# Softmax heads: q and k staged apart from V, DMA copies queued ahead of the weight load

## The chip, the core and the metric

The kernel runs on one core of a Trainium2 chip. The metric is the time of one execution on the device, in microseconds, from the first to the last instruction of the core. A core has TensorE (matmuls; its granted clock is 2.4 or 1.2 GHz), ScalarE, VectorE, GpSimd and SyncE, each with a queue of its own that it works off in order; they meet through semaphores.

## What is computed

One token sequence of 512 with width 1024 goes through a first block (stick-breaking attention with 8 heads, softmax attention with 8 heads and latent projections, "mla", gates, output projection) and two further layers, of which the first has a softmax attention with 16 heads and a forget term, "fox". The change touches both softmax attentions.

```python
def fox_attention(h, w_in, b_f, w_out):
    ...
    q = q * jnp.asarray(HEAD_DIM ** -0.5, q.dtype)
    f_logit = (proj[..., 3 * D:] + b_f).astype(jnp.float32)
    log_f = jax.nn.log_sigmoid(f_logit)
    c = lax.cumsum(log_f, axis=1).transpose(0, 2, 1)
    ...
        s = jnp.einsum('bhqd,bhkd->bhqk', qb, k, preferred_element_type=jnp.float32)
        s = s + cb[..., :, None] - c[..., None, :]
        q_pos = start + jnp.arange(Q_BLOCK)
        s = jnp.where(k_pos[None, :] <= q_pos[:, None], s, NEG_INF)
        pr = jax.nn.softmax(s, axis=-1)
        return jnp.einsum('bhqk,bhkd->bhqd', pr.astype(v.dtype), v)
```

The mla attention has the same form without the forget term, with 96 features for q and k, and a mask by chunks of 64.

## The kernel before

**Precision.** Every float32 operand is split into a high part, which ScalarE makes by casting to fp32r, and a low part, which VectorE makes by subtracting the high part from the value. A product is then three matmuls: high x high, high x low, low x high (L724 to L726, the helper `three`).

**Weights.** SyncE loads weight units of 1 MB into two raw slots (`load`, L490 to L494), in the order of a table. A load waits (L492, L493) until VectorE has split the unit that lay in the slot. In the attention stages the unit's two splits are cut into shares: w0 and w1 on ScalarE (L1214), c0 to c3 on VectorE (L1687); c0 waits for w1. Unit p+1 is split in pair p.

**Attention, in pairs of heads.** The softmax attentions work on two heads at a time, 4 pairs in mla and 8 in fox. `hh` 0 is the even head of a pair, 1 the odd one. Each engine follows an order written out by hand, a string of steps (`PE_FOX`, `ACT_FOX`, `DVE_FOX` and so on, the last two fox pairs `PE_LAST`, `ACT_LAST`, `DVE_LAST`). A step is a letter and a number:

- TensorE: z0 to z7 the score tiles (z0 to z3 of the even head, z4 to z7 of the odd one, L984 and L988), t0 to t7 the turns of the exponentials (L996), v0 and v1 the product with V, g0 to g7 the shares of a projection that runs beside the attention (6 matmuls a share).
- ScalarE: e0 to e7 exponentials (L1431), p0 to p7 high parts of the turned tiles (L1448), r0 and r1 inverse of the sums (L1438, L1440), w0 and w1 weight shares, s1 and s2 the staging of a head, o the output's high parts (L1371).
- VectorE: m0 to m7 row maxima (L2019), p0 to p7 low parts (L1723), g0 and g1 the output of a head (L1889), x0 and x1 the projection's output (L1879), c0 to c3 weight shares, s1 and s2 staging.

A score tile s uses PSUM bank s mod 3, so t(s) comes before z(s+3); v0 needs p3, v1 needs p7 of both ScalarE and VectorE; t(s) needs e(s) and VectorE's p(s-2).

**Staging** (`stage`, L1303 to L1318 on ScalarE, from L1833 on VectorE). Before a head's scores its q and k are cast (two ACTIVATE), then its V (a third); VectorE subtracts three times. q and k lie in one of two slots: the even head's in `head_qk`, the odd head's in spare rows of `act_b` (the other way round in mla). A slot is free when the scores of the head two before are done. V's place is free when the product with V of the head two before is done; ScalarE waits for it between the casts of k and V. s1 stages the odd head of this pair at the pair's start, s2 the even head of the next pair in its middle.

**Fox only: `copy_halves`** (L639 to L648). A head has 64 features; the free half of the partitions carries a second copy of the high part, and two rows carry the forget term. SyncE issues four DMAs a head: two of 64 x 512 (L645) and two of one row from `ssum` (L648). TensorE waits for all four before the head's first score tile (L975). The loop at L663 to L670 issues, for each pair, the copies of its odd head, the weight load that this pair allows, and the copies of the next even head.

Of the kernel before, what the change touches and what calls it, by code (L numbers as in the profile page):

```python
# [2394 lines left out]
```

## Time and profile before

| | us |
|---|---|
| median of 3 runs | 1895.83 |
| lowest and highest | 1895.67 and 1896.23 |
| the profiled execution | 1897.7 |
| its span, first to last instruction | 1895.9 |
| TensorE busy in it | 1770.2 (93%) |
| VectorE busy | 1069.8 (56%) |
| ScalarE busy | 739.6 (39%) |
| mean granted clock of TensorE | 0.975 of full |

The mla attention lies between about 325 and 414 us of the span, the fox attention between 567 and 804 us. Times in the rows below are counted from the span's start. A busy share is an average over stages with different limits; what ends a stage is read from the waits inside it. A timeline row merges equal instructions in a row (x2) and shows in brackets how long its engine was idle before it and what ended that.

### The profile page before, as it was taken

What the parts mean: (1) busy time and instruction counts of PE and PEld (TensorE: products, weight loads), DVE (VectorE), ACT (ScalarE), POOL (GpSimd) and SP (SyncE); (2) the same over time, 40 slices, a digit from 0 to 9 for tenths busy, and PEclk for the clock granted to TensorE, in tenths of its full rate; (3) what the DMA queues carried; (4) which work ended last, traced back from release to release, by engine and by line L of the source; (5) the groups of instructions that cost most, each with busy time, mean ns of one, the idle gap of its engine ahead of it and who ended that gap; (6) DMA issues with size and microseconds to landing.
All of it is one profiled execution on the core that took longest, in us unless ns stands there. A gap on an engine that the chain in (4) does not pass through costs nothing.

```text
span 1895.9 us, 22068 instructions
## 1 busy us (share of the span) xinstructions
PE 1770.2 (93%) x8332; PEld 1456.2 (77%) x8332; DVE 1069.8 (56%) x1394; ACT 739.6 (39%) x1073; POOL 179.3 (9%) x144
## 2 busy tenths in 40 slices
PE   8999999999897677899999999989999999999987
PEld 6978876888696566677888888667887788888866
DVE  6467767765555445667353444667555735444465
ACT  4266673663324434544122222453123412122245
POOL 2001110001200000022000000331002200000031
PEclk9999999999998888899999999989999999999999
DMA  7312123124231211213322322232231332232221
GB/s 241 98 45 66 58 58 100 45 69 132 67 96 40 60 41 39 73 56 111 103 97 89 109 91 78 67 100 94 89 106 56 111 108 93 89 111 89 78 68 66
DMA packets 166059, 160.48 MB, mean 85 GB/s; under 512 B 15137, under 2 KB 158782, under 8 KB 165726
## 3 DMA queue, kind: packets, MB, share of 16 engines
q1 hardware_dynamic: 165982, 159.42, 26.9%
q8 instruction: 52, 0.85, 0.2%
q14 instruction: 25, 0.20, 0.0%
HBM read 150.36 MB, written 4.19 MB: 82 GB/s over the span
## 4 chain that ended last, share of the span: by engine, by line
PE 68%; issue 12%; DVE 7%; POOL 4%; ACT 4%; DMA 3%; SPq 1%; POOLq 0%; DVEq 0%; ACTq 0%
PE bank L724 21%; PE bank L726 21%; PE bank L725 21%; POOL ssum L2325 3%; PE bank L984 2%; PE bank L996 1%; DMA head_qk<-ssum 1%; DVE split_weights L1679 1%; DVE work L1738 1%; DVE act_b L1723 1%; POOL tmp L2358 1%; DVE act_a L1725 1%; ACT split_weights L1205 1%; PE bank L988 1%; DMA raw_weights<-in_w_mlp_up 1%
## 5 line engine op out<-in xcount | busy, mean ns | idle before, releaser
L724 PE MATMUL bank<-act_a,split_weights 128*128 128x512 f32 x1392 | 558.1, 401 | 27.9 <-DVE act_a L1725 27.5
L726 PE MATMUL bank<-act_a,split_weights 128*128 128x512 f32 x1392 | 548.2, 394 | 0.0
L725 PE MATMUL bank<-act_a,split_weights 128*128 128x512 f32 x1392 | 548.1, 394 | 0.0
L1205 ACT ACTIVATE split_weights<-raw_weights 128x2048 fp32r<-128x2048 f32 (+1 forms) x119 | 223.7, 1880 | 345.3 <-PE bank L726 345.3
L1679 DVE TENSOR_TENSOR split_weights<-raw_weights,split_weights 128x2048 fp32r<-128x2048 f32 (+1 forms) x119 | 275.6, 2316 | 123.9 <-ACT split_weights L1205 120.5
L724 PEld LDWEIGHTS bank<-act_a,split_weights 128*128 128x128 f32 x1392 | 264.8, 190 | 93.8 <-issue 23.0
L726 PEld LDWEIGHTS bank<-act_a,split_weights 128*128 128x128 f32 x1392 | 263.9, 190 | 57.9
L725 PEld LDWEIGHTS bank<-act_a,split_weights 128*128 128x128 f32 x1392 | 264.6, 190 | 54.1 <-issue 2.2
L724 PE MATMUL bank<-act_b,split_weights 128*128 128x512 f32 x664 | 260.4, 392 | 0.0
L725 PE MATMUL bank<-act_b,split_weights 128*128 128x512 f32 x664 | 258.4, 389 | 0.0
L726 PE MATMUL bank<-act_b,split_weights 128*128 128x512 f32 x664 | 258.4, 389 | 0.0
L2329 POOL TENSOR_TENSOR ssum<-sq 128x512 f32<-128x512 f32 x16 | 28.0, 1749 | 1289.5 <-ACT sq L1235 1286.1
L725 PEld LDWEIGHTS bank<-act_b,split_weights 128*128 128x128 f32 x664 | 124.6, 188 | 27.0 <-issue 1.2
L724 PEld LDWEIGHTS bank<-act_b,split_weights 128*128 128x128 f32 x664 | 124.6, 188 | 26.8 <-issue 1.2
L726 PEld LDWEIGHTS bank<-act_b,split_weights 128*128 128x128 f32 x664 | 124.6, 188 | 26.0
L1547 ACT ACTIVATE act_b<-tmp 128x512 fp32r<-128x512 f32 x64 | 40.3, 632 | 229.2 <-DVE tmp L2186 227.9
L1235 ACT ACTIVATE sq<-work 128x512 f32<-128x512 f32 x117 | 71.0, 625 | 147.7 <-DVE work L2205 58.1
L2325 POOL TENSOR_TENSOR ssum<-ssum,sq 128x512 f32<-128x512 f32 x77 | 109.0, 1416 | 157.5 <-ACT sq L1235 149.2
L2186 DVE SCALAR_TENSOR_TENSOR tmp<-bank,rstd 128x512 f32<-128x512 f32 x64 | 43.5, 690 | 137.2 <-PE bank L726 136.2
L2205 DVE TENSOR_TENSOR work<-bank,work 128x512 f32<-128x512 f32 x48 | 32.9, 691 | 120.0 <-PE bank L726 120.0
L2019 DVE TENSOR_REDUCE negmax<-bank 128x1 f32<-128x128 f32 (+1 forms) x96 | 45.7, 485 | 77.0 <-PE bank L988 76.8
L1723 DVE TENSOR_TENSOR act_b<-tmp,act_b 128x512 fp32r<-128x512 f32 (+3 forms) x136 | 77.4, 603 | 10.7 <-ACT act_b L483 9.3
(188 smaller groups left out, 2081.1 us busy)
## 6 DMA issues: line engine op xcount, KB each, us to landing
raw_weights<-in_w_mlp_up SPq DMA_DIRECT2D x32, 1024.0 KB, 5.4
raw_weights<-in_w_mlp_down SPq DMA_DIRECT2D x32, 1024.0 KB, 5.1
raw_weights<-in_w_in SPq DMA_DIRECT2D x20, 1024.0 KB, 5.4
raw_weights<-in_w_conv_in SPq DMA_DIRECT2D x12, 1024.0 KB, 5.1
raw_weights<-in_w_attn_in SPq DMA_DIRECT2D x16, 512.0 KB, 4.7
raw_weights<-in_w_ple_gate SPq DMA_DIRECT2D x8, 1024.0 KB, 5.1
raw_weights<-in_w_out SPq DMA_DIRECT2D x4, 1024.0 KB, 5.1
raw_weights<-in_w_attn_in SPq DMA_DIRECT2D x4, 1024.0 KB, 5.2
```

Source lines behind the costliest of these rows:

```text
L724: nc.tensor.matmul(dst, w[0], a[0], start=first, stop=False)
L725: nc.tensor.matmul(dst, w[0], a[1], start=False, stop=False)
L726: mm = nc.tensor.matmul(dst, w[1], a[0], start=False, stop=last)
L984: nc.tensor.matmul(dst, qk(a)[0:width, j * P:(j + 1) * P], qk(b)[0:width, 0:cols], start=pass_ == 0, stop=False)
L1205: nc.scalar.activation(wsp[:, pl.slot, 0, pl.split_cols], raw[:, pl.slot, pl.raw_cols], ACT.Copy)\
L1235: nc.scalar.activation(sq[:, parity, :], src, ACT.Square).then_inc(sq_done, 1)
L1547: nc.scalar.activation(act_b[:, 0, 2 * j + m, :], tmp[:, m, :], ACT.Square)\
L1679: V.tensor_tensor(wsp[:, pl.slot, 1, cols], raw[:, pl.slot, pl.raw_cols], wsp[:, pl.slot, 0, cols].bitcast(F32), ALU.subtract).then_inc(w_ ...
L1723: V.tensor_tensor(dst, src, hi.bitcast(F32), ALU.subtract).then_inc(sem_, 1)
L2019: V.reduce_max(negmax[:, s:s + 1], score_bank(s, last)[:, 0:(s % TT + 1) * P], AX, negate=True)\
L2186: V.scalar_tensor_tensor(out=tmp[:, m, :], in0=done(pl, m)[:, :], scalar=0.0, in1=rstd[:, :], op0=ALU.max, op1=ALU.mult).then_inc(tile_rea ...
L2325: nc.gpsimd.tensor_tensor(ssum[:, :], ssum[:, :], sq[:, parity, :], ALU.add).then_inc(sq_added, 1)
```

## The change

It does three things. (1) The staging of q and k is a step of its own, that of V another. s2 and s3 stage q and k of the next pair's even and odd head as soon as the scores in the slot are done (z3 and z7); y1 and y2 stage V of this pair's odd head and of the next pair's even head. V gets semaphores of its own (`v_hi`, `v_staged`), for which the product with V waits. The first two heads' q and k are staged before the stage's loop. (2) `copy_halves` issues two DMAs a head in place of four: one for both copies (its source and target are two parts each, by `both_parts`) and one for the two rows. For that q's low part in fox goes to the other half of its slot. (3) In SyncE's loop the copies of the next even head stand ahead of the weight load, those of the next odd head behind it. All order strings of mla and fox are new but `PE_LAST`.

```diff
-        HI_STEPS = {"sb": 4, "mla": 3, "fox": 3}
+        HI_STEPS = {"sb": 4, "mla": 2, "fox": 2}
...
+        PE_MLA = "z0 g0 z1 g1 z2 t0 z3 t1 z4 g2 t2 z5 t3 z6 g3 v0 t4 z7 g4 t5 t6 g5 t7 g6 g7 v1"
+        ACT_MLA = "e0 e1 y1 p0 e2 p1 w0 e3 p2 p3 s2 w1 e4 e5 p4 y2 e6 p5 e7 p6 r0 p7 s3 r1"
...
-        PE_FOX = "z0 z1 z2 g0 g1 t0 z3 t1 g2 z4 t2 t3 z5 g3 t4 v0 z6 t5 z7 g4 g5 t6 t7 g6 g7 v1"
-        ACT_FOX = "s1 e0 e1 p0 e2 p1 e3 p2 p3 e4 e5 s2 p4 p5 w0 e6 e7 r0 p6 p7 w1 r1"
-        DVE_FOX = "m0 m1 m2 s1 m3 p0 p1 m4 p2 p3 m5 s2 m6 p4 m7 p5 c0 c1 g0 p6 p7 x0 c2 x1 c3 g1"
+        PE_FOX = "z0 z1 g0 g1 z2 t0 z3 t1 z4 g2 t2 g3 t3 z5 g4 t4 z6 z7 v0 t5 g5 t6 t7 g6 g7 v1"
+        ACT_FOX = "w0 e0 e1 w1 p0 e2 p1 s2 e3 e4 p2 y1 p3 e5 s3 e6 p4 p5 e7 r0 p6 y2 p7 r1"
+        DVE_FOX = "m0 m1 c0 c1 m2 p0 m3 m4 p1 c2 s2 c3 p2 p3 m5 m6 m7 y1 p4 p5 g0 p6 p7 x0 y2 x1 s3 g1"
...
-        ACT_LAST = ("s1 e0 e1 e2 o0 p0 w0 e3 o1 p1 p2 o2 w1 e4 e5 p3 s2 e6 p4 r0 e7 p5 p6 p7 o3 r1",
+        ACT_LAST = ("e0 e1 e2 y1 o0 p0 w0 e3 o1 p1 p2 o2 s2 w1 e4 e5 p3 e6 p4 s3 r0 e7 p5 y2 p6 p7 o3 r1",
...
+        def both_parts(hh, second):
+
+            if hh:
+                rows = act_b[:, :, 4:6, :]
+                return rows[:, :, 0, :] if second == 2 else act_b[:, :, :, :].rearrange("p a k n -> p (a k) n")[:, 4:14:9, :]
+            return head_qk[:, 0:second + 1:second, :]
...
-                qk, (own, other) = qk_parts("fox", hh), halves(hh)
+                own, other = halves(hh)
                 sp.wait_ge(ATT["fox"]["stage_hi"], HI_STEPS["fox"] * h + 2)
-                for dst, src in ((qk(0)[other, :], qk(0)[own, :]), (qk(3)[own, :], qk(2)[own, :])):
-                    sp.dma_start(dst.bitcast(F32), src.bitcast(F32)).then_inc(halves_copied[hh], 16)
-                for part in range(2):
-                    row, to = 32 * part + h, other.start + part
-                    sp.dma_start(qk(3)[to:to + 1, :].bitcast(F32), ssum[row:row + 1, :]).then_inc(halves_copied[hh], 16)
+                dst, src = both_parts(hh, 3)[other, :, :], both_parts(hh, 2)[own, :, :]
+                sp.dma_start(dst.bitcast(F32), src.bitcast(F32)).then_inc(halves_copied[hh], 16)
+                sp.dma_start(qk_parts("fox", hh)(3)[own.start:own.start + 2, :].bitcast(F32), ssum[h:h + 33:32, :])\
+                    .then_inc(halves_copied[hh], 16)
...
             copy_halves(0)
+            copy_halves(1)
             load_qk(Place(tab, "fox_qk_next", 2), 4)
-            for pair in range(FOX_HEADS // 2):
-                copy_halves(2 * pair + 1)
+            for pair in range(FOX_HEADS // 2 - 1):
+                copy_halves(2 * pair + 2)
                 if pair < 3:
                     load_qk(Place(tab, "fox_qk_next", 3 + pair), 5 + pair)
                 elif pair < 5:
                     load_out(Place(tab, "fox_out", pair - 3), pair - 3)
-                if pair < FOX_HEADS // 2 - 1:
-                    copy_halves(2 * pair + 2)
+                copy_halves(2 * pair + 3)
...
                 def values(i, hh):
                     pe.wait_ge(A["pt_ready"], 8 * i + 4 * hh + 4)
                     pe.wait_ge(A["gathered"], FREE + 2 * i + hh)
+                    pe.wait_ge(A["v_staged"], 2 * i + hh + 1)
```

SyncE's queue at pair 0, where `fox_qk_next` 3 is loaded: `raw_weights` is the load (two issues), `act_b` the odd head's slot, `head_qk` the even head's. Before:

```order
L494 DMA raw_weights<-in_w_attn_in 128x8x128 [waits w_split]
L494 DMA raw_weights<-in_w_attn_in 128x8x128
L645 DMA head_qk<-head_qk 64x512 [waits fox_stage_hi]
L645 DMA head_qk<-head_qk 64x512
L648 DMA head_qk<-ssum 1x16x32 x2
L645 DMA act_b<-act_b 64x512 [waits fox_stage_hi]
L645 DMA act_b<-act_b 64x512
L648 DMA act_b<-ssum 1x16x32 x2
```
After, the same load and its neighbours:

```order
L652 DMA head_qk<-head_qk 64x2x512 [waits fox_stage_hi]
L653 DMA head_qk<-ssum 2x512
L501 DMA raw_weights<-in_w_attn_in 128x8x128 [waits w_split]
L501 DMA raw_weights<-in_w_attn_in 128x8x128
L652 DMA act_b<-act_b 64x2x512 [waits fox_stage_hi]
L653 DMA act_b<-ssum 2x512
```
Before, the copies of both heads of the next pair stand behind the load that waits for `w_split`; now the even head's stand ahead of it and the odd head's behind it, two issues a head for four.

ScalarE in a fox pair, the staging of the next even head: L1312 and L1313 cast q and k, L1318 V, L1448 is a p step. Before (s2 p4 p5):

```order
L1308 ISA
L1312 ISA [waits fox_scores]
L1312 ACTIVATE head_qk<-work 64x512
L1313 ISA
L1313 ACTIVATE head_qk<-work 64x512
L1318 ISA [waits fox_out]
L1318 ACTIVATE head_v<-work 128x4x64
L1446 REGISTER_ALU [waits fox_turned]
L1448 ACTIVATE act_b<-bank 128x128 [waits fox_out]
L1448 ACTIVATE act_b<-bank 128x2x128 [waits fox_turned]
```
After, the staging of the next odd head (L1319, L1320), which did not exist here, ahead of e6, p4, p5 and e7 (s3 e6 p4 p5):

```order
L1315 ISA
L1319 ISA [waits fox_scores]
L1319 ACTIVATE act_b<-work 64x512
L1320 ISA
L1320 ACTIVATE act_b<-work 64x512
L1442 REGISTER_ALU
L1443 ACTIVATE tmp<-bank,negmax 128x384 [waits fox_negmax]
L1458 REGISTER_ALU [waits fox_turned]
L1460 ACTIVATE act_b<-bank 128x128 [waits fox_out]
L1460 ACTIVATE act_b<-bank 128x2x128 [waits fox_turned]
```
V's cast with its wait for `fox_out` no longer stands behind those of q and k; the wait of s3 for `fox_scores` (z7) stands ahead of e6.

VectorE in a fox pair: L1687 (after: L1706) is a c step. Before (m7 p5 c0 c1 g0 p6 p7), L2019 an m step, L1889 a g step, near the pair's end:

```order
L2019 TENSOR_REDUCE negmax<-bank 128x1 [waits fox_scores]
L1723 TENSOR_TENSOR act_b<-bank,act_b 128x2x128 [waits fox_pt_hi]
L1685 REGISTER_ALU
L1687 TENSOR_TENSOR split_weights<-raw_weights,split_weights 128x512 [waits w_hi]
L1687 TENSOR_TENSOR split_weights<-raw_weights,split_weights 128x512
L1884 REGISTER_ALU
L1889 TENSOR_TENSOR work<-bank,sq 64x512 [waits fox_sum_inverse,fox_out]
L1723 TENSOR_TENSOR act_b<-bank,act_b 128x3x128 [waits fox_pt_hi]
L1723 TENSOR_TENSOR act_b<-bank,act_b 128x4x128 [waits fox_pt_hi]
```
After, at the pair's start (m0 m1 c0 c1 m2 p0 m3):

```order
L2043 TENSOR_REDUCE negmax<-bank 128x1 [waits fox_scores]
L2042 REGISTER_ALU
L2043 TENSOR_REDUCE negmax<-bank 128x1 [waits fox_scores]
L1704 REGISTER_ALU
L1706 TENSOR_TENSOR split_weights<-raw_weights,split_weights 128x512 [waits w_hi]
L1706 TENSOR_TENSOR split_weights<-raw_weights,split_weights 128x512
L2042 REGISTER_ALU
L2043 TENSOR_REDUCE negmax<-bank 128x1 [waits fox_scores]
L2048 REGISTER_ALU
L1742 TENSOR_TENSOR act_b<-bank,act_b 128x128 [waits fox_pt_hi]
L2042 REGISTER_ALU
L2043 TENSOR_REDUCE negmax<-bank 128x1 [waits fox_scores]
```
The first two c steps, which wait for `w_hi` (w1 on ScalarE), moved from ahead of g0, p6 and p7 to ahead of m2.

## Rows read from the trace of the kernel before

**Rows 1.** Waits of TensorE, 560 to 757 us: waiter, releaser, us, times, longest.

```profile
PE bank L984 <- DMA head_qk<-ssum: 38.8, 5, 8.2
PE bank L724 <- DVE act_b L1723: 11.6, 6, 1.9
```

**Rows 2.** Stretches: length, busy us of each engine (instructions), granted clock, DMA share, GB/s.

```profile
325.15:414.30 89.15, 88.68 (x495) 76.38 (x496) 61.62 (x122) 55.35 (x110) 0.00 (x0) 1.00 0.14 45
567.43:757.02 189.59, 139.17 (x696) 118.48 (x697) 92.49 (x179) 84.39 (x166) 0.00 (x0) 0.86 0.17 45
757.02:804.00 46.98, 37.31 (x193) 30.80 (x192) 28.94 (x57) 27.98 (x59) 0.00 (x0) 0.89 0.26 74
```

**Rows 3.** Waits of SyncE's queue, 560 to 800 us, columns as in Rows 1.

```profile
SPq L493 <- DVE split_weights L1687: 126.1, 5, 27.2
```

**Rows 4.** Timeline of SyncE's queue: start, us, line, DMA, count.

```profile
657.99 1.00 SPq L494 DMA_DIRECT2D raw_weights<-in_w_attn_in  x2
...
660.72 1.24 SPq L648 DMA_DIRECT2D head_qk<-ssum  x2
...
744.96 1.14 SPq L645 DMA_DIRECT2D head_qk<-head_qk  x2
```

**Rows 5.** DMA issues of the whole run: count, KB each, median us to landing.

```profile
head_qk<-head_qk SPq DMA_DIRECT2D x16, 128.0 KB, 4.8
...
head_qk<-ssum SPq DMA_DIRECT2D x16, 2.0 KB, 4.1
act_b<-ssum SPq DMA_DIRECT2D x16, 2.0 KB, 2.3
```

**Rows 6.** Timeline of TensorE, pair 1 and two later starts: start, us, line, [idle before].

```profile
632.05 0.80 PE L984 MATMUL bank<-head_qk 128*128 128x256 f32 x2 [7.99 <-DMA head_qk<-ssum]
...
643.98 0.48 PE L724 MATMUL bank<-act_b,head_v 128*128 128x512 f32 x1
...
646.00 0.51 PE L984 MATMUL bank<-act_b 128*128 128x384 f32 x2
...
655.66 0.49 PE L724 MATMUL bank<-act_b,head_v 128*128 128x512 f32 x1 [1.93 <-DVE act_b L1723]
...
666.06 0.79 PE L984 MATMUL bank<-head_qk 128*128 128x256 f32 x2 [8.21 <-DMA head_qk<-ssum]
...
757.02 0.40 PE L984 MATMUL bank<-head_qk 128*128 128x256 f32 x2
```

**Rows 7.** Stretches from z0 to t0, columns as in Rows 2; last the five after a wait.

```profile
567.43:571.48 4.05, 4.05 (x22) 3.50 (x23) 3.07 (x6) 2.15 (x5) 0.00 (x0) 1.00 0.29 65
...
632.05:638.79 6.74, 6.74 (x22) 5.75 (x22) 3.07 (x6) 0.84 (x2) 0.00 (x0) 0.56 0.00 0
...
sum 31.96, PE 31.95 PEld 27.41 DVE 15.37 ACT 4.20 POOL 0.00; mean PE 6.39 PEld 5.48 DVE 3.07 ACT 0.84 POOL 0.00
```

**Rows 8.** Timeline of ScalarE in pair 1, columns as in Rows 6.

```profile
644.46 0.62 ACT L1312 ACTIVATE head_qk<-work 64x512 fp32r x1
...
646.30 0.42 ACT L1318 ACTIVATE head_v<-work 128x256 fp32r x1 [0.70 <-PE bank L726]
...
648.12 1.16 ACT L1431 ACTIVATE tmp<-bank,negmax 128x384 f32<-128x384 f32 x2
649.31 0.60 ACT L1438 ACTIVATE sq<-bank 64x512 f32<-64x512 f32 x1
...
650.59 1.00 ACT L1448 ACTIVATE act_b<-bank 128x384 fp32r<-128x384 f32 x2
651.49 1.05 ACT L1214 ACTIVATE split_weights<-raw_weights 128x1024 fp32r<-128x1024 f32 x1
```

**Rows 9.** Timeline of VectorE in pair 1, columns as in Rows 6.

```profile
652.58 1.29 DVE L1687 TENSOR_TENSOR split_weights<-raw_weights,split_weights 128x512 fp32r<-128x512 f32 x2 [3.69 <-ACT split_weights L1214]
...
654.39 1.14 DVE L1723 TENSOR_TENSOR act_b<-bank,act_b 128x384 fp32r<-128x384 f32 x2
...
659.24 0.68 DVE L1889 TENSOR_TENSOR work<-bank,sq 64x512 f32 x1 [1.32 <-ACT sq L1440]
```

More of the change, by code:

```diff
@@ L1423, in _ @@
                     stage("mla", 0, 0, first=True)
+                    stage_values("mla", 0, 0, ATT["mla"]["v_hi"], first=True)
             def softmax_attention(kind, heads):
@@ L1452, in two_pairs @@
                         pair = 2 * i + a
+                        first = False
                         for what, s in steps(orders[a]):
                             if what == "s":
+                                if not (last and a == 1):
+                                    stage(kind, pair + 1, s % 2)
+                            elif what == "y":
                                 if not (last and a == 1 and s == 2):
-                                    stage(kind, pair + s // 2, s % 2)
+                                    stage_values(kind, pair + s // 2, s % 2, A["v_hi"], first=first and s == 1)
                             elif what == "w" and orders is ACT_LAST:
@@ L1477, in _ @@
             act.wait_ge(tile_read, tab.end[tab.first["kv_up"]])
+            stage("mla", 0, 1, first=True)
             softmax_attention("mla", MLA_HEADS)
@@ L1509, in _ @@
                     stage("fox", 0, 0, first=True)
+                    stage_values("fox", 0, 0, ATT["fox"]["v_hi"], first=True)
+                    stage("fox", 0, 1, first=True)
             act.wait_ge(tile_read, tab.end[tab.first["fox_v"] + 3])
@@ L1842, in stage @@
                 own, other = (slice(0, QK), None) if kind == "mla" else halves(hh)
-                q_lo = qk(0)[other, :] if kind == "sb" else qk(1)[own, :]
+                q_lo = {"sb": qk(0), "mla": qk(1), "fox": qk(1)}[kind][own if kind == "mla" else other, :]
                 k_lo = qk(2)[other, :] if kind == "fox" else qk(3)[own, :]
@@ L1848, in stage, with values_lo, rest_halves @@
                 low(k_lo, k, qk(2)[own, :], A["staged"])
-                dve.wait_ge(A["stage_hi"], before + HI_STEPS[kind])
-                low(head_v[:, hh, 1, :, 0:HD], head_values(kind, i, hh), head_v[:, hh, 0, :, 0:HD], A["staged"])
-            def rest_halves(part, value):
+                if kind == "sb":
+                    values_lo(kind, i, hh, A["stage_hi"], before + HI_STEPS[kind], A["staged"])
+            def values_lo(kind, i, hh, hi_done, count, lo_done):
+                dve.wait_ge(hi_done, count)
+                low(head_v[:, hh, 1, :, 0:HD], head_values(kind, i, hh), head_v[:, hh, 0, :, 0:HD], lo_done)
+            def rest_halves(part, value, which):
                 for hh in range(2):
-                    V.memset(qk_parts("sb", hh)(part)[halves(hh)[1], :].bitcast(F32), value)
+                    V.memset(qk_parts("sb", hh)(part)[halves(hh)[which], :].bitcast(F32), value)
             def clear_padding():
@@ L2038, in two_pairs @@
                             if what == "s":
+                                if not (last and a == 1):
+                                    stage(kind, pair + 1, s % 2)
+                            elif what == "y":
                                 if not (last and a == 1 and s == 2):
-                                    stage(kind, pair + s // 2, s % 2)
+                                    h = 2 * pair + s
+                                    values_lo(kind, pair + s // 2, s % 2, A["v_hi"], h + 1, A["v_staged"])
                             elif what == "g":
@@ L2141, in _ @@
                     stage("fox", 0, 0)
+                    values_lo("fox", 0, 0, ATT["fox"]["v_hi"], 1, ATT["fox"]["v_staged"])
+                    stage("fox", 0, 1)
             dve.wait_ge(tile_read, tab.end[tab.first["fox_v"] + 3])
@@ L2362, in _ @@
             sum_squares(KT)
-            pool.wait_ge(ATT["fox"]["staged"], 3 * FOX_HEADS)
+            for copied in halves_copied:
+                pool.wait_ge(copied, 32 * FOX_HEADS // 2)
             OUTPUTS_AT = {"mlp0": 8, "ple_gate0": 16, "conv_in": 0, "mlp1": 8, "ple_gate1": 16}
```

36 lines of the change are left out of this document (19 added, 17 removed).

## The prediction

> **What bounds the kernel now.** I read the waits of TensorE first, then the table of stretches, the queue that issues the DMAs, and last the timelines of one pair of forget-attention heads. The reader should see four things.
>
> First, in the first six pairs (0 to 5) TensorE's matmuls are stopped by two things: 38.8 us in 5 waits for a DMA that writes head_qk from ssum, and 11.6 us in 6 waits of 1.93 us for VectorE's p7 [rows 1, 6]. Second, these pairs take 189.59 us at a mean granted clock of 0.86; the MLA stage before runs at 1.00 and TensorE is busy for 88.68 of its 89.15 us [rows 2], so it has nothing to give. Third, SyncE's queue is strictly in order. Five times, 126.1 us in total, it stands at the weight load (L493, L494) that waits for VectorE's split of the raw slot it overwrites [rows 3], and the copies of the next even head are queued behind it: the load goes at 657.99 us, the row copies only at 660.72 us, and TensorE starts at 666.06 us. After pair 5, with no load in between, the same copies go at 744.96 us, twelve microseconds early, and z0 at 757.02 us has no wait [rows 4, 6]. The load's data are in the way too: row copies into head_qk (even heads, most of them behind a load) land after 4.1 us at the median, those into act_b (odd heads) after 2.3 us [rows 5]. Fourth, after each such wait the clock is at its lower level, 1.2 GHz, for some microseconds: the work from z0 to t0 takes 4.05 us in pair 0, at clock 1.00, but 31.96 us in the five pairs after a wait, at 0.56 in the one shown [rows 7].
>
> **The sum, part by part.** It is made in the profiled execution, whose span is 1895.9 us; the median of the timed runs is 1895.83 us, so differences are taken off the median as they are.
>
> 1. The even head's copies move ahead of the load and wait for s2's two casts alone. Those begin 12.4 us after z0 now (644.46 against 632.05 us) [rows 6, 8]; in the new order s2 stands right after p1, and I find it done about 8 us after z0. Two issues of 0.6 us and a landing of at most 4.8 us [rows 5] put the data there at about 14 us. They are due at 21. The wait goes, 38.8 us; what is late next is the end of v1, where z0 already stands without a wait at 757.02 us.
> 2. With the waits goes the slow stretch behind them: 31.96 - 5 x 4.05 = 11.7 us [rows 7], supposing that TensorE stays busy as in pair 0.
> 3. The waits before v1. VectorE's c0 stands 3.69 us for w1, the second half of ScalarE's weight cast, which comes behind e6, e7, r0, p6 and p7; g0, p6 and p7 are queued behind c0 on VectorE [rows 8, 9]. In the new order w0 and w1 stand at the head of the pair. Is p7 in time then? From z0, TensorE's steps to the end of z7 are 11.8 us of work (z0, z1, z2, g0 and g1 are the 4.05 us above), 12.3 with the waits of point 4. ScalarE's s3 waits for exactly that. Then s3 1.0, e6 0.5, p4 0.2, and p5, which needs t5, from 14.7 on; p5 0.35, e7 0.6, r0 1.2, p6 0.4, y2 0.35, p7 0.55 [rows 8] end at 18.1, VectorE's p7 at 18.8 [rows 9]. TensorE, from 12.3: v0 2.0 (643.98 to 646.00 us [rows 6]), t5 0.2, g5 1.4, t6 and t7 0.7, g6 and g7 2.8: v1 is due at 19.4. Slack 0.6 us. The wait goes, but barely: 11.6 us.
> 4. New waits at t2 and t3. c0 and c1, 1.3 us [rows 9], now stand ahead of m2 and wait for w1, which ends 4.4 us after z0 (r1 1.3, w0 1.0, then e0 and e1 behind g1 and m0, m1, then w1 1.0 [rows 8]). So m2 ends at 6.1 and e2 at 6.8, where t2 is due at 6.6; and e3, behind p1 and s2 (1.4 us), ends at 8.9, where t3 is due at 8.6. That is 0.5 us in each of six pairs, 3.0 us given back, between 0 (a step a little shorter) and 6.
> 5. Staging costs no more work. s3's subtractions on VectorE stand between x1 and g1 at the pair's end, 1.4 us, hidden by v1 (2.0 us on TensorE) and by ScalarE's r1, for which g1 stands idle 1.32 us now [rows 9]. Without that cover m0 would be later, but t0 is not due before 4.0 us and e0 ends at 3.0. Nothing.
> 6. The first two heads are staged among the V tiles of fox_v: two more casts on ScalarE, 1.4 us more on VectorE, where most V tiles wait for TensorE. Nothing; the bound is 1.4 us.
> 7. Fewer, larger copies, one of 128 KB x 2 for two and one of two rows for two. No row shows their shape; with landings from 2.3 to 4.8 us [rows 5] for smaller ones and 7 us to spare, nothing.
> 8. Pairs 6 and 7, with their own orders: 46.98 us, of which TensorE is busy 37.31 [rows 2]. ScalarE no longer starts the pair with three casts, so t0 comes 0.4 us and p0's low part about 1 us earlier. But in pair 6 the casts of s2 now stand ahead of w1, e4, e5 and p3, which puts v0 some 0.9 us later, and s3 waits for z7 ahead of r0 and e7, which puts v1 0.8 us later. Pair 7 gains about 0.7 us. Net 0; the ends are half of the 9.7 idle us gained, 5 us, and 3 us lost.
> 9. MLA: no copies there. The same walk finds every step in time, the closest g0 right behind z0, which needs x1 of the pair before, with 1 us of slack. Nothing; the bound is 0.5 us a pair, 2 us lost.
>
> Sum: 38.8 + 11.7 + 11.6 - 3.0 = 59.1 us. Cross-check on one pair: 632.05 to 666.06 us is 34.0, less 8.2, 1.9 and 6.74 - 4.05 = 2.7 is 21.2 us [rows 6, 7], 21.7 with the new waits; 6 x 21.7 = 130.2, and 189.6 - 130.2 = 59.4. **1895.8 - 59.1 = 1836.7 us.**
>
> **Rivals.** A: the wait before v1 stays. For it: 0.6 us of slack, out of some twenty durations and hand-overs, and s3's wait for z7, a new obstacle in ScalarE's queue. Against: VectorE's 3.69 us for w1 is gone. Price 11.6 us: 1848.3 us.
>
> B: the block in SyncE's queue only moves to the odd head, whose copies stand behind the load in the new order. If c3 still came as late as now, just at the pair's end, two load issues of 0.5, two copies of 0.6 and a landing of 4.1 us [rows 4, 5] end 6.3 us into the next pair, where z4 is due at 5.0: 1.3 us in five pairs, 6.5 us, about 1843 us. Against: c3 now follows s2 and comes at about 10 us, so the load is through before s3 casts. The Trainium skill (DMA: Bandwidth & Descriptors, section Queues, rings and completion order) says that each DMA engine consumes the descriptors of one queue in the order of its ring; the rule speaks against putting anything behind a load, and the 4.1 against 2.3 us agree with it.
>
> C, on the other side: ScalarE's queue becomes the bound. s3 holds e6, p4, p5, e7, r0, p6 and p7 until z7 is scored; a late z7 makes v1 late, and the next pair's z7 with it. To be slower by over 0.2% (3.8 us) it needs 62.9 us of new waits, 7.9 us in each of the eight pairs. My slack would have to be off by more than that in a pair of 21.7 us in which the casts, exponentials and copies of ScalarE are busy for about 14. It decides only from there; the rows speak strongly against it. About 1903 us.
>
> D: the change doesn't do what it says, since s2 or its copies are late for another reason and z0 still waits. Then 11.6 - 3.0 us go: 1887 us. The copies after pair 5, free of a load, were twelve microseconds early, which speaks against it.
>
> **How the numbers follow.** Forecast 0.68, around 1836.7 us, from 1829 (5 us of pairs 6 and 7 gone, no new waits) to 1846 (3 us lost there, 3 more at t2 and t3, 2 in MLA, 1.4 at the start). A 0.20, B 0.06, C 0.03, D 0.03. The range takes in A and B: 1829 to 1849 us. What a measurement of this kernel can tell from no change is about 0.2%, 3.8 us. All cases but C are faster by more, 0.97; of C a third falls within it, 0.01; slower 0.02.
>
> **What would show it.** In the profile after: no wait of TensorE for a DMA in pairs 1 to 5, granted clock 1.00 from the first z0 of the stage to pair 6, z0 to z0 21.7 us (23.1 with the old wait before v1, rival A), waits at t2 and t3 of 0.2 to 0.3 us for ScalarE, the copies of an even head issued some 8 us after z0 and the load behind them at about 10. B would show as a wait at z4 for a DMA into act_b, C as waits of several microseconds for ScalarE in every pair. I am wrong if pairs 0 to 5 take more than 136 us.

## The result, and the profile after

The changed kernel takes 1837.99 us at the median (1837.1 to 1839.91, 4 runs) where the kernel before takes 1895.92 in the same session (1895.67 to 1896.23, 4 runs): a ratio of 0.9696, with a 95% interval of 0.9679 to 0.9713. The forecast was 1836.7 us, with a range of 1829 to 1849. The profiled execution took 1837.41 us, its span is 1835.6 us, the mean granted clock 0.986. Its span is 60.3 us shorter than that of before; the medians differ by 57.9, because the profiled execution of before (1897.7 us) lay 1.8 us above that median of 1895.92, and this one 0.6 us below its own.

Stretches of the kernel after: length, busy us of each engine (instructions), granted clock, DMA share, GB/s. The lines answer to [rows 2]: the MLA stage, pairs 0 to 5 of fox, pair 6, and pair 7 up to its last product with V.

```profile
324.90:414.30 89.40, 89.18 (x501) 77.69 (x502) 62.08 (x122) 56.11 (x112) 0.00 (x0) 1.00 0.16 51
566.32:692.79 126.47, 125.65 (x696) 107.17 (x697) 91.63 (x179) 82.98 (x166) 0.00 (x0) 1.00 0.26 67
692.79:721.25 28.46, 18.77 (x88) 15.17 (x87) 17.55 (x34) 15.87 (x32) 0.00 (x0) 0.82 0.09 20
721.25:742.40 21.15, 18.77 (x107) 15.83 (x106) 10.94 (x22) 11.22 (x24) 0.00 (x0) 1.00 0.39 125
```

Pairs 0 to 5 took 189.59 us at a clock of 0.86; now they take 126.47 at 1.00, that is 63.1 us less. Of this 49.6 are waits (50.4 before, 0.8 left) and 13.5 are TensorE's own time, 139.17 to 125.65 us for the same 696 matmuls, with the clock at 1.00 in place of 0.86. TensorE is busy for 99% of the stretch now, so there is next to nothing left in it. The rest nearly cancels: the stage begins 1.1 us earlier, pair 7 is 0.3 us shorter up to v1, pair 6 is 3.0 us longer, and what follows pair 7's v1 is 1.3 us longer. 63.1 + 1.1 + 0.3 - 3.0 - 1.3 = 60.3 us, up to rounding.

What TensorE still waits for from 566 to 692 us (waiter, releaser, us, times, longest), to set beside [rows 1]:

```profile
PE bank L990 <- DVE work L1796: 0.9, 1, 0.9
PE bank L1002 <- ACT tmp L1443: 0.6, 3, 0.2
```

The 38.8 us for the DMA and the 11.6 us for VectorE's p7 are gone, both to the last one. The first line is the stage's first score tile, outside of the pairs. SyncE's queue, from 560 to 740 us, beside [rows 3]:

```profile
SPq L652 <- ACT head_qk L1320: 101.0, 7, 16.6
SPq L500 <- DVE split_weights L1706: 4.2, 5, 0.8
```

It still stands for a long time, but at the copies, waiting for q's and k's casts, which is no loss as long as they come in time. At the weight load it stands for 4.2 us where it stood for 126.1. The queue and TensorE in pair 3 (after's L652 and L653 are the copies, L501 the load, L990 scores, L1002 turns, L730 the product with V):

```profile
637.51 0.64 SPq L652 DMA_DIRECT2D head_qk<-head_qk  x1
638.19 0.52 SPq L653 DMA_DIRECT2D head_qk<-ssum  x1
639.60 0.92 SPq L501 DMA_DIRECT2D raw_weights<-in_w_attn_out  x2
642.98 0.64 SPq L652 DMA_DIRECT2D act_b<-act_b  x1
```
```profile
629.31 0.40 PE L990 MATMUL bank<-head_qk 128*128 128x256 f32 x2
...
636.23 0.55 PE L1002 MATMUL bank<-consts,tmp 128*128 128x128 f32 x3 [0.20 <-ACT tmp L1443]
...
641.51 0.39 PE L730 MATMUL bank<-act_b,head_v 128*128 128x512 f32 x1
...
648.58 0.39 PE L730 MATMUL bank<-act_b,head_v 128*128 128x512 f32 x1
...
650.51 0.40 PE L990 MATMUL bank<-head_qk 128*128 128x256 f32 x2
```
VectorE's p6 and p7 in the same pair:

```profile
646.83 1.33 DVE L1742 TENSOR_TENSOR act_b<-bank,act_b 128x384 fp32r<-128x384 f32 x2
```

The even head's copies go 8.2 us after z0 and the load 10.3 us after it. v1 starts 19.3 us after z0, and VectorE's p7 ends at 648.16, 0.42 us before it. The whole pair takes 21.2 us, to the next z0 at 650.51. Compare [rows 4, 6], where z0 to z0 took 34.0 us. (What those rows call pair 1, with its z0 at 632.05 us, is pair 2 by the count from 0: the z0 of pairs 0 and 1 are at 567.43 and 598.53 us. Nothing in the sum depends on it.)

**Pair 6** is the one place that lost. Before, its v1 began 23.5 us after its z0. t7 and v1 in the kernel before (pair 6 began at 757.02 us [rows 6]):

```profile
777.14 0.63 PE L996 MATMUL bank<-consts,tmp 128*128 128x128 f32 x4 [0.68 <-DVE act_b L1723]
...
780.49 0.50 PE L724 MATMUL bank<-act_b,head_v 128*128 128x512 f32 x1 [1.33 <-DVE act_b L1723]
```

After, it begins 26.4 us after it. TensorE and ScalarE in pair 6 of after:

```profile
692.79 0.40 PE L990 MATMUL bank<-head_qk 128*128 128x256 f32 x2
...
705.86 0.79 PE L730 MATMUL bank<-act_b,head_v 128*128 128x512 f32 x1 [1.09 <-DVE act_b L1742]
...
715.86 1.09 PE L1002 MATMUL bank<-consts,tmp 128*128 128x128 f32 x4 [2.61 <-DVE act_b L1742]
...
719.22 0.50 PE L730 MATMUL bank<-act_b,head_v 128*128 128x512 f32 x1
```
```profile
711.57 0.63 ACT L1319 ACTIVATE act_b<-work 64x512 fp32r<-64x512 f32 x1 [1.85 <-PE bank L994]
712.11 0.61 ACT L1320 ACTIVATE act_b<-work 64x512 fp32r<-64x512 f32 x1
712.74 0.59 ACT L1450 ACTIVATE sq<-bank 64x512 f32<-64x512 f32 x1
713.37 0.63 ACT L1452 ACTIVATE sq<-sq 64x512 f32<-64x512 f32 x1
714.03 0.69 ACT L1443 ACTIVATE tmp<-bank,negmax 128x512 f32<-128x512 f32 x1
714.61 0.38 ACT L1460 ACTIVATE act_b<-bank 128x256 fp32r<-128x256 f32 x1
```

s3 (the first two lines) stands idle for 1.85 us until z7 is scored, with r0, e7 and p5 behind it. VectorE's p5 follows at 715.31 us, and t7 at 715.86 waits 2.61 us for it. After z0, t7 comes 2.95 us later than before. On TensorE g2 stands between t7 and v1. Before, the two took 2.02 us at a granted clock of 1.00, and 1.33 us of idle time followed ahead of v1, which could have taken up a part of the lateness. After, behind the wait of 2.61 us, they run at a granted clock of 0.54 and take 3.36 us. So no wait shows at v1, and it is late by the whole 3.0 us.

### The profile page after: what moved, and what is told of

Its sections match the earlier page's. It is cut to its first block, busy times and chain, and to the rows that moved or that the text cites. A ratio compares the mean times of both kernels' runs of the same rounds, so it can differ in the third digit from the quotient of the medians.

```text
span 1835.6 us, 22028 instructions
## 1 busy us (share of the span) xinstructions
PE 1758.6 (96%) x8332; PEld 1447.8 (79%) x8332; DVE 1070.2 (58%) x1394; ACT 738.8 (40%) x1073; POOL 180.1 (10%) x144
## 4 chain that ended last, share of the span: by engine, by line
PE 68%; issue 13%; DVE 7%; ACT 5%; POOL 5%; DMA 2%; POOLq 0%; SPq 0%; DVEq 0%; ACTq 0%
PE bank L730 21%; PE bank L732 21%; PE bank L731 21%; POOL ssum L2357 3%; PE bank L990 1%; PE bank L1002 1%; DVE split_weights L1698 1%; DVE work L1757 1%; POOL tmp L2390 1%; DVE act_a L1744 1%; ACT split_weights L1212 1%; DMA raw_weights<-in_w_mlp_up 1%; DMA raw_weights<-in_w_ple_gate 1%; ACT sq L1242 1%; POOL ssum L2361 0%
## 5 line engine op out<-in xcount | busy, mean ns | idle before, releaser
L730 PE MATMUL bank<-act_a,split_weights 128*128 128x512 f32 x1392 | 556.5, 400 | 26.2 <-DVE act_a L1744 25.8
L730 PEld LDWEIGHTS bank<-act_a,split_weights 128*128 128x128 f32 x1392 | 263.4, 189 | 90.4 <-issue 23.1
L730 PE MATMUL bank<-act_b,split_weights 128*128 128x512 f32 x664 | 260.4, 392 | 0.0
L730 PEld LDWEIGHTS bank<-act_b,split_weights 128*128 128x128 f32 x664 | 124.6, 188 | 26.9 <-issue 1.2
L1258 ACT ACTIVATE act_a<-work,gains 128x512 fp32r<-128x512 f32 x56 | 40.1, 721 | 64.6 <-DVE work L1764 30.3
```

The lines of the kernel that those rows point to most:

```text
L730: nc.tensor.matmul(dst, w[0], a[0], start=first, stop=False)
L1258: nc.scalar.activation(act_a[:, 0, k, :], wt(X + k), ACT.Copy, scale=col(gain + k))\
```

## The experiments

In all of them the kernel before ran on the same chip: 1897.1 us at the median beside the queue's order alone, the weight shares alone, the load put back and the late shares; 1896.94 beside the two edits together, the four copies and the first two kernels of pair 6; 1896.61 beside the last three.

### The queue's order alone

```diff
                 copy_halves(2 * pair + 1)
+                if pair < FOX_HEADS // 2 - 1:
+                    copy_halves(2 * pair + 2)
                 if pair < 3:
...
-                if pair < FOX_HEADS // 2 - 1:
-                    copy_halves(2 * pair + 2)
```


> The kernel before with one edit: SyncE issues the copies of the next even head ahead of the weight load. Staging, orders and four copies a head stay. Theory (the queue position alone holds z0 back): the five waits of 7 to 8 us and the slow stretches go, 38.8 + 11.7 = 50.5 us, and the 1.93 us before each v1 stay, since they hang on the weight shares: about 1845.4 us. Rival 1 (the copies also need the earlier staging of q and k): z0 still waits, more than 1860 us. Rival 2 (all waits have the same cause): about 1834 us.

Measured: 1853.72 us (1852.45 to 1855.78), ratio 0.9775 (0.9759 to 0.9792). All waits for the DMA at z0 are gone. What is left in pairs 0 to 5, as stretches (columns as above) and waits of TensorE, and the landing of the copies (count, KB each, median us):

```profile
567.82:712.65 144.83, 131.87 (x696) 113.40 (x697) 91.34 (x179) 83.89 (x166) 0.00 (x0) 0.95 0.22 59
588.72:613.17 24.45, 21.15 (x116) 17.88 (x117) 15.29 (x31) 14.19 (x28) 0.00 (x0) 1.00 0.26 65
613.17:624.00 10.83, 10.83 (x55) 9.80 (x56) 7.35 (x15) 5.37 (x12) 0.00 (x0) 0.84 0.46 121
```
```profile
PE bank L724 <- DVE act_b L1723: 11.6, 6, 1.9
PE bank L984 <- DMA act_b<-ssum: 1.4, 1, 1.4
```
```profile
head_qk<-head_qk SPq DMA_DIRECT2D x16, 128.0 KB, 2.3
...
head_qk<-ssum SPq DMA_DIRECT2D x16, 2.0 KB, 1.8
```

The order in the queue removes the wait by itself, as the theory has it, but 8 us less came of it than expected. The six 1.93 us waits before v1 remain, and behind most of them the clock falls: 613.17 us is the start of v1 after such a wait, and the 10.83 us from there have a clock of 0.84, and so have those behind the next three; 588.72 is the same place a pair earlier, and there it stays at 1.00. A pair at clock 1.00 has 21.15 us of TensorE's own time; six of them would be 126.9 us, and there are 131.87, so 5.0 us are the low clock behind short waits. In the kernel before, the long wait follows two microseconds of work later, so the lower clock there falls into idle time and into the stretch behind z0, which my 11.7 us counted; that this is why it shows only now is my reading, not a measurement. With z4's wait of 1.4 us, which is new, that is 6.4 of the 8 us. The copies land after 2.3 and 1.8 us where they took 4.8 and 4.1 behind the load [rows 5].

### The weight shares alone

```diff
-        ACT_FOX = "s1 e0 e1 p0 e2 p1 e3 p2 p3 e4 e5 s2 p4 p5 w0 e6 e7 r0 p6 p7 w1 r1"
-        DVE_FOX = "m0 m1 m2 s1 m3 p0 p1 m4 p2 p3 m5 s2 m6 p4 m7 p5 c0 c1 g0 p6 p7 x0 c2 x1 c3 g1"
+        ACT_FOX = "w0 s1 e0 e1 w1 p0 e2 p1 e3 p2 p3 e4 e5 s2 p4 p5 e6 e7 r0 p6 p7 r1"
+        DVE_FOX = "m0 m1 m2 s1 c0 c1 m3 p0 p1 m4 c2 p2 c3 p3 m5 s2 m6 p4 m7 p5 g0 p6 p7 x0 x1 g1"
```


> The kernel before with w0, w1 and c0 to c3 moved from the end of a fox pair to its start, nothing else; the weight load still stands ahead of the even head's copies. Theory: what blocks the queue is not the order of the issues but the late c3 for which the load waits; with c3 at about 9 us into the pair the load passes early, the copies are in time and the wait before v1 is gone too: 62 us less, some 3 to 4 us given back because e0 now stands behind w0 and the three staging casts: about 1837.5 us. Rival (the place ahead of the load is what counts): z0 keeps its 7 to 8 us, and only the 11.6 us before v1 go, about 1884 us.

Measured: 1841.51 us (1841.37 to 1841.95), ratio 0.971 (0.9694 to 0.9726). Two strings of the kernel before, with the staging, the four copies and the queue as they were, bring 55.6 us, where the whole change brings 57.9, each against before in its own session. In pair 1 the load is issued at 598.04 us, 10.4 us after z0 (before, in the same pair: 624.20 us, 25.7 us after it), and TensorE never waits at z0. Its waits from 567 to 700.27 us:

```profile
PE bank L996 <- ACT tmp L1431: 2.4, 5, 0.5
PE bank L984 <- DMA act_b<-ssum: 1.7, 5, 0.6
PE bank L996 <- DVE act_b L1723: 0.3, 2, 0.2
```

The first two come from s1: the odd head is staged at the pair's start, ahead of e0, so that t0 waits 0.48 us, and its copies just miss z4. In the changed kernel, which has w0 ahead of e0 as well but no s1, both waits are gone. Pairs 0 to 5 take 133.7 us against 126.5. Of the difference 3.6 us is idle time and 3.3 us TensorE's busy time, at a clock of 1.00. About 1.2 of the 3.3 go with the order of TensorE's steps (six pairs of before's order are 126.9 us, six of the new one 125.65); the other 2.0 lie in pairs 1 to 5, and I can't name their cause from the records. No run separates the split of the staging from the new order strings: the 3.5 us between this kernel and the change belong to the two together.

### The two edits together

```diff
+                if pair < FOX_HEADS // 2 - 1:
+                    copy_halves(2 * pair + 2)
                 if pair < 3:
...
-        ACT_FOX = "s1 e0 e1 p0 e2 p1 e3 p2 p3 e4 e5 s2 p4 p5 w0 e6 e7 r0 p6 p7 w1 r1"
+        ACT_FOX = "w0 s1 e0 e1 w1 p0 e2 p1 e3 p2 p3 e4 e5 s2 p4 p5 e6 e7 r0 p6 p7 r1"
...
```
DVE_FOX is changed as in the kernel before this one.

> The kernel before with two edits together: the weight shares w0, w1 and c0 to c3 at the pair's start, and the even head's copies ahead of the weight load. Alone the first gave 1841.5 us, the second 1853.7. My theory: the two edits act on the same wait (z0 behind a load that waits for c3) and do not add; once c3 is early the load is through before the copies come, and what is left of the first kernel (0.48 us at t0 and 0.24 to 0.6 us at z4 in each pair, from the casts of the odd head at the pair's start) is not in SyncE's queue. 1841.5 us, within 1 us. Rival: they add in part, the z4 wait for a DMA goes since the weight data are elsewhere then, and the time comes to 1838 to 1839, the changed kernel's.

Measured: 1842.57 us (1840.95 to 1843.1), ratio 0.9716 (0.9699 to 0.9732), 1.1 us above the expectation and no gain over the shares alone. The edits do not add: each removes the same 38.8 us. The waits are those of the shares alone, z4's among them:

```profile
614.88 0.33 PE L996 MATMUL bank<-consts,tmp 128*128 128x128 f32 x1 [0.48 <-ACT tmp L1431]
617.72 0.48 PE L984 MATMUL bank<-act_b 128*128 128x256 f32 x2 [0.32 <-DMA act_b<-ssum]
```

### The changed kernel with the load put back ahead

```diff
-                copy_halves(2 * pair + 2)
                 if pair < 3:
...
                     load_out(Place(tab, "fox_out", pair - 3), pair - 3)
+                copy_halves(2 * pair + 2)
                 copy_halves(2 * pair + 3)
```


> The changed kernel with the weight load put back ahead of the even head's copies. Theory: with c3 about 10 us into the pair the load no longer blocks; the copies go at about 11.5 us instead of 8 and land before 17, due at 21: the same time within 0.1%, 1838 us, no wait for a DMA. Rival (the place in the queue is what made the gain): waits at z0 come back, up to 50 us more.

Measured: 1837.33 us (1837.0 to 1837.6), ratio 0.9687 (0.9671 to 0.9704), the same as the change. SyncE's queue stands at the load again, five times and 80.1 us, and TensorE waits for no DMA:

```profile
SPq L500 <- DVE split_weights L1706: 80.1, 5, 16.5
```

A long stand of a queue costs nothing as long as it ends in time. With c3 early, the order in the queue, the part of the change that I put first in the sum, buys nothing.

### The changed kernel with the shares at their late places

```diff
-        ACT_FOX = "w0 e0 e1 w1 p0 e2 p1 s2 e3 e4 p2 y1 p3 e5 s3 e6 p4 p5 e7 r0 p6 y2 p7 r1"
-        DVE_FOX = "m0 m1 c0 c1 m2 p0 m3 m4 p1 c2 s2 c3 p2 p3 m5 m6 m7 y1 p4 p5 g0 p6 p7 x0 y2 x1 s3 g1"
+        ACT_FOX = "e0 e1 p0 e2 p1 s2 e3 e4 p2 y1 p3 e5 s3 e6 p4 p5 w0 e7 r0 p6 y2 p7 w1 r1"
+        DVE_FOX = "m0 m1 m2 p0 m3 m4 p1 s2 p2 p3 m5 m6 m7 y1 p4 p5 c0 c1 g0 p6 p7 x0 y2 c2 x1 c3 s3 g1"
```


> The changed kernel with w0, w1 and c0 to c3 at about the places they had before (w0 behind p5, w1 behind p7; c0, c1 ahead of g0, c2, c3 around x1), nothing else. Theory: VectorE's c0 waits for w1 again, g0, p6 and p7 behind it, so v1 waits 1.5 to 2 us in each of six pairs, 9 to 12 us; and the odd head's copies, behind a load that waits for c3 at the pair's end, make z4 wait 1.3 to 2 us in five pairs, 6 to 10 us: 1853 to 1860 us, and no wait at z0. Rival 1 (the odd head's copies are in time in any case): only the v1 waits, 1847 to 1850 us. Rival 2 (the places of the shares don't matter once q and k are staged early): 1838 us.

Measured: 1878.14 us (1873.56 to 1879.04), ratio 0.9894 (0.9878 to 0.9911), 40 us above the change. Pairs 0 to 5 and TensorE's waits in them:

```profile
566.70:731.01 164.31, 138.12 (x696) 117.11 (x697) 90.99 (x177) 83.92 (x166) 0.00 (x0) 0.92 0.20 52
```
```profile
PE bank L730 <- DVE act_b L1742: 19.8, 6, 3.3
PE bank L990 <- DMA act_b<-ssum: 4.7, 4, 1.5
PE bank L1002 <- ACT tmp L1443: 1.7, 6, 0.3
```

This is what rivals A and B describe, both at once. With c0 waiting for a late w1, v1 waits 3.3 us in every pair, more than the 1.93 us of before. A likely reason is s3, which in pair 2 stands 0.82 us for z7 and casts for 1.2 us ahead of p4, p5, w0 and the rest; I read that from ScalarE's rows, and no run isolates it. And the odd head's copies behind a late load make z4 wait 0.9 to 1.5 us in four pairs. The waits are 26 us, and 12.5 us are TensorE's own time at a clock of 0.92. My expectation had the waits at their old size and the clock at full speed, and was 18 to 25 us too low. The kernel is also 24.4 us slower than before's staging with the queue's order alone (1853.7 us in the same session): with late shares the new staging and its strings cost time, and only the early shares make them pay.

### Four copies a head

```diff
-                dst, src = both_parts(hh, 3)[other, :, :], both_parts(hh, 2)[own, :, :]
-                sp.dma_start(dst.bitcast(F32), src.bitcast(F32)).then_inc(halves_copied[hh], 16)
...
+                for to, fr in ((0, 0), (3, 2)):
+                    sp.dma_start(qk(to)[other, :].bitcast(F32), qk(fr)[own, :].bitcast(F32)).then_inc(halves_copied[hh], 16)
+                for part in range(2):
...
```


> The changed kernel, with the four copies a head of the kernel before in place of the two: nothing else differs. My theory: the copies of an even head are issued some 8 us after z0 and are due at 21 us, those of an odd head some 14 us after z0 and due five us into the next pair; two issues more (1.2 us of SyncE's queue) reach neither due time. 1838 us, within 1.5 us, no wait of TensorE for a DMA. Rival: the larger copies are part of the gain, because the four issues make the queue late; then a wait for a DMA appears at z4 or z0, and the time is 3 us or more longer.

Measured: 1837.14 us (1837.02 to 1837.4), ratio 0.9687 (0.967 to 0.9703). The same; two more issues a head fit in.

### Pair 6: s3 behind p7

```diff
-        ACT_LAST = ("e0 e1 e2 y1 o0 p0 w0 e3 o1 p1 p2 o2 s2 w1 e4 e5 p3 e6 p4 s3 r0 e7 p5 y2 p6 p7 o3 r1",
+        ACT_LAST = ("e0 e1 e2 y1 o0 p0 w0 e3 o1 p1 p2 o2 s2 w1 e4 e5 p3 e6 p4 r0 e7 p5 y2 p6 p7 s3 o3 r1",
-        DVE_LAST = ("m0 m1 m2 m3 y1 p0 o0 m4 p1 m5 o1 p2 p3 c0 m6 s2 o2 c1 p4 m7 g0 c2 p5 s3 c3 p6 y2 p7 o3 g1",
+        DVE_LAST = ("m0 m1 m2 m3 y1 p0 o0 m4 p1 m5 o1 p2 p3 c0 m6 s2 o2 c1 p4 m7 g0 c2 p5 c3 p6 y2 p7 s3 o3 g1",
```


> As the kernel with both steps moved in pair 6, but s2 stays where the change has it, and only s3 moves behind p7. My theory: s3's wait for z7 is the larger part, about 2.1 us (from r0 at 712.74 us to 710.8, the 2 us that p5 and t7 lose); s2 is worth the other 0.4 to 1 us at v0. 1835.9 us, between 1835 and 1837. Rival: s2 is what makes this pair late, as my prediction put it (0.9 us at v0); then this kernel stays at 1838 and only the one with both moved gains.

Measured: 1833.91 us (1833.09 to 1835.29), ratio 0.9669 (0.9653 to 0.9685). TensorE in pair 6 of this kernel:

```profile
705.87 0.79 PE L730 MATMUL bank<-act_b,head_v 128*128 128x512 f32 x1 [1.23 <-DVE act_b L1742]
...
714.12 0.63 PE L1002 MATMUL bank<-consts,tmp 128*128 128x128 f32 x4 [0.68 <-DVE act_b L1742]
...
716.16 0.50 PE L730 MATMUL bank<-act_b,head_v 128*128 128x512 f32 x1
```

t7's wait falls from 2.61 to 0.68 us, and t7 comes 1.74 us earlier. t7 and g2 then take 2.04 us at a granted clock of 1.00, not 3.36, which is another 1.32. So v1 comes 3.06 us earlier, while v0 stays where it was. s3 was the cause, and all of the loss against before (3.0 us) comes back.

### Pair 6: both steps moved

```diff
-        ACT_LAST = ("e0 e1 e2 y1 o0 p0 w0 e3 o1 p1 p2 o2 s2 w1 e4 e5 p3 e6 p4 s3 r0 e7 p5 y2 p6 p7 o3 r1",
+        ACT_LAST = ("e0 e1 e2 y1 o0 p0 w0 e3 o1 p1 p2 o2 w1 e4 e5 p3 s2 e6 p4 r0 p5 e7 p6 p7 s3 y2 o3 r1",
-        DVE_LAST = ("m0 m1 m2 m3 y1 p0 o0 m4 p1 m5 o1 p2 p3 c0 m6 s2 o2 c1 p4 m7 g0 c2 p5 s3 c3 p6 y2 p7 o3 g1",
+        DVE_LAST = ("m0 m1 m2 m3 y1 p0 o0 m4 p1 m5 o1 p2 p3 c0 m6 o2 c1 p4 m7 p5 g0 s2 c2 p6 c3 p7 s3 y2 o3 g1",
```


> The changed kernel, but in pair 6 alone (the first string of ACT_LAST and DVE_LAST) s2 stands behind p3 on ScalarE as in the kernel before, and s3 at the end, behind p7, in place of ahead of r0. My theory: the changed kernel loses 3 us in pair 6 because s3 waits there for z7 and holds r0, e7 and p5, whose low part t7 needs, and because s2 holds w1, e4, e5 and p3, which v0 needs. With both out of the way the 2.61 us wait at t7 shrinks to about 0.5 and v1 comes 2 to 3 us earlier: 1835.2 us, between 1834 and 1836. Rival: the wait before v0 or another step takes it up, since TensorE is at its low clock there for other reasons, and v1 stays: 1838 us.

The strings also move p5 ahead of e7 on ScalarE and of g0 on VectorE, and y2 behind s3 on both.

Measured: 1834.56 us (1833.78 to 1835.35), ratio 0.9673 (0.9657 to 0.9689). TensorE, and VectorE ahead of its p7:

```profile
704.78 0.79 PE L730 MATMUL bank<-act_b,head_v 128*128 128x512 f32 x1 [1.10 <-DVE act_b L1742]
...
716.32 0.50 PE L730 MATMUL bank<-act_b,head_v 128*128 128x512 f32 x1 [1.88 <-DVE act_b L1742]
```
```profile
711.88 0.67 DVE L1913 TENSOR_TENSOR work<-bank,sq 64x512 f32<-64x512 f32 x1
712.59 0.68 DVE L1744 SCALAR_TENSOR_TENSOR head_qk<-work,head_qk 64x512 fp32r<-64x512 f32 x1
713.19 0.68 DVE L1742 TENSOR_TENSOR head_qk<-work,head_qk 64x512 fp32r<-64x512 f32 x1
...
715.58 0.68 DVE L1742 TENSOR_TENSOR act_b<-bank,act_b 128x512 fp32r<-128x512 f32 x1
```

Against the kernel with s3 alone moved, v0 gains 1.1 us and v1 nothing. From m7 at 710.94 us to the end of p7 at 716.26 VectorE has no idle time, and s2's two subtractions (1.3 us) now stand in that row, between g0 and p6. So p7, which v1 needs, ends late, and a new wait of 1.88 us takes the gain back.

### Pair 6: s3 behind p7, and s2 moved on ScalarE only

The changed kernel and the one with s3 behind p7 ran once more beside this one, so that a few microseconds can be told.

> The changed kernel as it is, beside the two that follow, so that a few us can be compared on one chip. 1837.6 us, within 1 us of its median of 1837.99 us and of the kernel with the load first (1837.33 us).

> The changed kernel with s3 behind p7 in pair 6 once more, beside the changed kernel. 3 us below it, as its profile has it (v1 of pair 6 starts at 716.16 us of the span in place of 719.22): 1834.5 us. Rival: the 4 us between the medians were partly drift between two sessions; then 2 us or less.

Measured: 1838.06 us (1837.44 to 1840.56, 5 runs) and 1834.43 us (1833.96 to 1835.04, 5 runs). The difference is 3.6 us, so it was no drift between sessions.

```diff
-        ACT_LAST = ("e0 e1 e2 y1 o0 p0 w0 e3 o1 p1 p2 o2 s2 w1 e4 e5 p3 e6 p4 s3 r0 e7 p5 y2 p6 p7 o3 r1",
+        ACT_LAST = ("e0 e1 e2 y1 o0 p0 w0 e3 o1 p1 p2 o2 w1 e4 e5 p3 s2 e6 p4 r0 e7 p5 y2 p6 p7 s3 o3 r1",
-        DVE_LAST = ("m0 m1 m2 m3 y1 p0 o0 m4 p1 m5 o1 p2 p3 c0 m6 s2 o2 c1 p4 m7 g0 c2 p5 s3 c3 p6 y2 p7 o3 g1",
+        DVE_LAST = ("m0 m1 m2 m3 y1 p0 o0 m4 p1 m5 o1 p2 p3 c0 m6 s2 o2 c1 p4 m7 g0 c2 p5 c3 p6 y2 p7 s3 o3 g1",
```


> In pair 6 s3 stands behind p7, and s2 behind p3 on ScalarE, but on VectorE s2 keeps the place that the change gave it. With s2 moved on VectorE too, v0 began 1.1 us earlier (704.78 against 705.87 us), and a wait of 1.88 us before v1 took it all back, since s2's two subtractions stood between g0 and p6. With VectorE's s2 ahead of o2 the v0 gain should reach v1: 1.0 us below the kernel with only s3 moved, 1833.5 us. Rival: t7's or v1's wait comes back and takes the 1.0 us, as before; then the two are equal.

Measured: 1833.07 us (1832.72 to 1833.78, 5 runs), ratio to before 0.9666 (0.9652 to 0.9679). Every run of it is below every run of the kernel with s3 alone moved beside it (1833.96 to 1835.04), though not below those of the session before (from 1833.09). At the median it is 1.4 us below that kernel, where 1.0 was expected, and 5 us below the changed kernel: the fastest of this study.

```profile
705.25 0.79 PE L730 MATMUL bank<-act_b,head_v 128*128 128x512 f32 x1 [1.10 <-DVE act_b L1742]
...
715.90 0.50 PE L730 MATMUL bank<-act_b,head_v 128*128 128x512 f32 x1
```

Its pair 6 begins at 693.19 us, so v0 comes 12.1 us after z0 and v1 22.7, against 13.1 and 23.4 with s3 alone moved and 13.1 and 26.4 in the change.

## Why the prediction was right, point by point

The time was right, and each large wait went as forecast. Two terms were mis-sized, in opposite directions, and one reading of the cause was too narrow.

1. **The even head's copies: 38.8 us.** Right: no wait is left, copies at 8.2 and load at 10.3 us after z0 where I had 8 and 10. But I tied the term to the queue's order, and either of two parts brings it: the order alone (1853.7 us) or the early shares alone (1841.5 us); in the finished kernel the order is worth nothing (1837.3 us with it undone). In the sum this changes nothing, in the advice it changes all.
2. **The slow stretch behind the waits: 11.7 us.** TensorE's own time fell by 13.5. By the 21.15 us of a pair of before's order at clock 1.00, 12.3 of it is the clock (139.17 - 126.9); the other 1.2 go with the new order of TensorE's steps (126.9 to 125.65), and I had no term for them. The term holds only because the waits before v1 went too: in the kernel with the queue's order alone 5.0 us of low clock stay behind those.
3. **The waits before v1: 11.6 us.** Right, and as narrow as walked: v1 due 19.4 us after z0 and started at 19.3, with a slack of 0.42 us for the 0.6 forecast. In the kernel with late shares the waits are 3.3 us each, 19.8 in all, and the clock falls behind them. The 11.6 us that I put on rival A are the waits alone and leave out what the clock behind them costs, 5.0 us in the kernel with the queue's order alone.
4. **New waits at t2 and t3: 3.0 us given back.** Mis-sized: 0.6 us, 0.2 at t2 in pairs 1, 3 and 5, and none at t3. I had counted two waits of 0.2 to 0.3 us in each of six pairs. In pair 1, e2 ended 6.9 us after z0, about as walked (6.8), but t2 was due 6.7 us after z0, where I had 6.6; and t3 started at 8.8 without a wait, where I had it held until 8.9.
5. **Staging on VectorE, points 5 to 7.** Right: nothing shows. Four copies a head in place of two gave 1837.1 us.
6. **Pairs 6 and 7 (point 8): net 0.** This is the step that failed: measured 2.7 us lost, inside the bound of 3 but by another path. I walked the chain from s3 to VectorE's p7 and set its end against v1, 0.8 us late. The step that needs the chain first is t7, which waits for p5, and it waits 2.61 us where it waited 0.68. So the lateness lands at t7, where I did not look, and behind that wait t7 and g2 ran at a clock of 0.54 for 1.3 us more, a term that I did not have. With s3 out of the way both come back, 1.74 and 1.32 us. s2 was sized well: moving it makes v0 1.0 us earlier (0.9 forecast), and in the change v0 is only 0.4 us later than before because t0 comes 0.4 us and p0 about 1 us sooner, or so I read it. Pair 7 gained 0.3 us for the 0.7 forecast.
7. **MLA (point 9).** Right: 89.40 us against 89.15 [rows 2].

The errors against the span: the sum had 1.8 us too little for TensorE's own time, 2.2 too much for the new waits (3.0 for 0.8 of idle time) and nothing for the 1.1 at the stage's start, against 2.7 for pairs 6 and 7 and 1.3 after them: 59.1 became 60.3. That they nearly cancel is luck, and so is a part of the 1.3 us between forecast and median. Against the median's 57.9 the sum was 1.2 us too large, as the span of a profiled execution at 1897.7 us, from which I took the differences, was set beside a median of 1895.8.

Of the rivals, A and B did not come, and the kernel with late shares shows both waits: B priced z4's wait at 1.3 us, and it measured 0.9 to 1.5. The rule of the Trainium skill that I cited beside B (DMA: Bandwidth & Descriptors, section Queues, rings and completion order), that the descriptors of one queue are consumed in order, fits what the copies did once they stood ahead of the load: 2.3 and 1.8 us to landing in place of 4.8 and 4.1. The weight shares alone and the two edits together differ by that order only, and there these copies land after 2.8 and 1.8 us (those from `ssum`). In the changed kernel the order is worth no time, since the copies are due long after. C and D did not come; the 1903 us that I gave C has no working, 1836.7 + 62.9 would be 1899.6.

## What to carry to other kernels

When a queue stands at a wait and something urgent is behind it, there are two cures, to reorder the queue or to make the awaited step early; do one at a time, because together they hide which of them pays. The early step can bring more, since it frees what else waits behind it (here p7, by 11.6 us). Follow a late chain to the first step that needs any link of it, not to the last, and look at what stands behind that step on its engine. And a step that was moved ahead for the sake of a steady loop should be walked once more in the pairs with orders of their own: the strings of one pair here held 5 us.
